# The RWKV recurrence of a diffusion step: 64x64 blocks per head in diagonal quarters of TensorE, written out without its loop

## The reference, cut to what matters

```python
def wkv7_scan(r, w, k, v, kk, a, s0, reverse):
    def step(s, inp):
        r_t, w_t, k_t, v_t, kk_t, a_t = inp
        sa = jnp.einsum('bhvk,bhk->bhv', s, -kk_t)
        s = s * w_t[:, :, None, :] + sa[..., None] * (kk_t * a_t)[:, :, None, :] + v_t[..., None] * k_t[:, :, None, :]
        return s, jnp.einsum('bhvk,bhk->bhv', s, r_t)
    xs = tuple(jnp.moveaxis(t, 1, 0) for t in (r, w, k, v, kk, a))
    s_fin, y = lax.scan(step, s0, xs, reverse=reverse)
    return jnp.moveaxis(y, 0, 1), s_fin
```

## Time and profile before

| | us |
|---|---|
| median of 3 runs (6167.9 to 6171.29) | 6169.99 |
| span of the profiled execution | 6159.2 |
| PE busy | 4924.3 (80%) |
| DVE busy | 1753.6 (28%) |
| ACT busy | 898.5 (15%) |
| POOL busy | 494.2 (8%) |

### The profile page before, as it was taken

How to read it: one execution, slowest core, us unless ns; L and a number is a source line. 1 busy time by engine, 2 the same in 40 slices (tenths; PEclk the granted TensorE clock), 3 DMA queues, 4 the chain that set the end, 5 groups by cost and what they waited for, 6 DMA issues and landing times. The chain is left out here.

```text
span 6159.2 us, 76147 instructions
## 1 busy us (share of the span) xinstructions
PE 4924.3 (80%) x31726; PEld 4331.8 (70%) x31726; DVE 1753.6 (28%) x2068; ACT 898.5 (15%) x1195; POOL 494.2 (8%) x284
## 2 busy tenths in 40 slices
PE   4799999963289999963516579984999999999990
PEld 1799999951189999951106434454999999999990
DVE  3200100037533333335466623334000000000006
ACT  0111111112122222212422300000000000000000
POOL 1100000003211011111101000000000000000003
PEclk6899999975589999986755789985999999999995
DMA  8422222113311111125853162225777777777755
GB/s 316 140 64 67 65 71 64 58 54 117 110 29 31 27 28 32 32 73 206 306 146 80 49 222 82 82 90 193 262 251 264 240 260 251 261 261 249 264 175 219
DMA packets 517520, 891.70 MB, mean 145 GB/s; under 512 B 149102, under 2 KB 321642, under 8 KB 498394
## 3 DMA queue, kind: packets, MB, share of 16 engines
q1 hardware_dynamic: 478596, 794.19, 38.1%
q0 software_dynamic: 5808, 38.93, 2.5%
q10 hardware_dynamic: 32964, 56.31, 2.5%
HBM read 747.98 MB, written 141.35 MB: 144 GB/s over the span
## 5 line engine op out<-in xcount | busy, mean ns | idle before, releaser
L2430 PE MATMUL ex_bank<-ex_xT,ex_ring 128*128 128x144 f32 x8192 | 1029.6, 287 | 9.5 <-DVE ex_yT L2538 9.0
L2430 PEld LDWEIGHTS ex_bank<-ex_xT,ex_ring 128*128 128x128 f32 x8192 | 1013.2, 190 | 13.8 <-issue 12.2
L379 PE MATMUL feat_acc<-proj_hH,feat_wH 128*128 128x384 f32 x2112 | 706.7, 335 | 12.6 <-DVE feat_wL L362 12.6
L379 PE MATMUL feat_acc<-proj_hL,feat_wH 128*128 128x384 f32 x2112 | 706.4, 334 | 0.0
L379 PE MATMUL feat_acc<-proj_hH,feat_wL 128*128 128x384 f32 x2112 | 706.4, 334 | 0.0
L2444 PE MATMUL ex_bank<-ex_act,ex_ring 128*128 128x144 f32 x4096 | 537.3, 297 | 0.0
L2444 PEld LDWEIGHTS ex_bank<-ex_act,ex_ring 128*128 128x128 f32 x4096 | 533.8, 200 | 0.6
L2059 PE MATMUL op_acc<-op_w,op_yT 128*128 128x512 f32 x1152 | 497.3, 595 | 25.2 <-DMA op_w<-in_w_out 25.2
L2059 PEld LDWEIGHTS op_acc<-op_w,op_yT 128*128 128x128 f32 x1152 | 219.8, 191 | 302.2 <-issue 302.2
L379 PEld LDWEIGHTS feat_acc<-proj_hH,feat_wH 128*128 128x128 f32 x2112 | 397.2, 188 | 13.0 <-DVE feat_wL L362 13.0
L379 PEld LDWEIGHTS feat_acc<-proj_hL,feat_wH 128*128 128x128 f32 x2112 | 397.3, 188 | 0.0
(11 more groups left out here) (403 smaller groups left out, 6220.9 us busy)
## 6 DMA issues: line engine op xcount, KB each, us to landing
ex_ring<-in_w_gate SPq DMA_DIRECT2D x256, 512.0 KB, 3.7
ex_ring<-in_w_up SPq DMA_DIRECT2D x256, 512.0 KB, 4.5
ex_ring<-in_w_down SPq DMA_DIRECT2D x256, 512.0 KB, 4.4
lru_wq<-in_w_mod SPq DMA_DIRECT2D x64, 1024.0 KB, 11.6
proj_raw<-in_w_in SPq DMA_DIRECT2D x43, 1024.0 KB, 5.5
mod_slab<-in_w_mod SPq DMA_DIRECT2D x8, 4096.0 KB, 31.0
scratch_FEAT<-feat_out ACTq DMA_DIRECT2D x43, 576.0 KB, 2.8
rr_bdt<-scratch_RW SPq DMA_DIRECT2D x288, 64.0 KB, 2.4
```

Source lines behind the costliest of these rows:

```text
L379: last = pe.matmul(acc[k][:, g, 0:SEG], a[:, k, t, :], b[:, t, cols], start=t == 0 and j == 0, stop=t == KT - 1 and j == 2)
L2430: last = pe.matmul(bank[b][:, n * C:(n + 1) * C], ring[:, k % RING, h * FE + f * P:h * FE + (f + 1) * P], xT[:, k, :], start=k == 0 and n ...
```

## The change

Each head is computed as its own 64x64 block. A matmul of head h uses partitions 64h to 64h + 63 of its operands and `tile_position=(64 * h, 64 * h)`, so the two heads of a pair use two diagonal quarters of the array and write the two halves of the same PSUM columns. The zeros are gone: buffers are 128x256 per direction, `bdt` becomes `src`, loaded by 8 DMAs a chunk and never cleared. Products are joined where both halves fit one bank: T and Tt, X and Y of a level, kT and bT (now `kb`), each with one eviction of 512 columns; there are 19 products instead of 25. Transposes become matmuls with a unit matrix `eye` as the moving operand. POOL makes X1 and Y1 in one operation. The masks become compact, with their content the same. The loop over pairs of chunks is written out on every engine. The exchange of states uses one DMA each way.

```diff
 PRODUCTS = [
-    ("T", "dve", ""), ("Tt", "dve", ""), ("Bt", "dve", ""), ("A2", "dve", ""), ("W2", "dve", "T Tt"),
-    ("X2", "act", "W2 Tt"), ("Y2", "act", "W2 Tt"), ("W4", "dve", "X2"), ("X4", "act", "W4 Y2"), ("Y4", "act", "W4 Y2"),
-    ("W8", "dve", "X4"), ("X8", "act", "W8 Y4"), ("Y8", "act", "W8 Y4"), ("W16", "dve", "X8"), ("vT", "act", ""),
-    ("X16", "act", "W16 Y8"), ("Y16", "act", "W16 Y8"), ("W32", "dve", "X16"), ("R", "dve", "Bt vT -S"),
-    ("Y32", "act", "W32 Y16"), ("kT", "act", ""), ("U", "dve", "R Y32"), ("bT", "act", ""), ("Yo", "act", "U A2 vT -S"),
-    ("S", "dve", "U bT kT vT"),
+    ("T", "dve", ""), ("Bt", "dve", ""), ("A2", "dve", ""), ("W2", "dve", "T"),
+    ("XY2", "act", "W2"), ("vT", "act", ""), ("W4", "dve", "XY2"), ("XY4", "act", "W4"),
+    ("W8", "dve", "XY4"), ("XY8", "act", "W8"), ("W16", "dve", "XY8"),
+    ("kb", "act", ""), ("XY16", "act", "W16"), ("R", "dve", "Bt vT -S"), ("W32", "dve", "XY16"),
+    ("Y32", "act", "W32"), ("U", "dve", "R Y32"), ("Yo", "act", "U A2 vT -S"), ("S", "dve", "U kb vT"),
 ]
...
-        masks = s.sb("masks", [P, 2, 9, P])
+        eye = s.sb("eye", [P, RC])
+        masks = s.sb("masks", [P, 2, 9, RC])
         pc = s.sb("pc", [P, 2, NJ_A, T // RC])
-        S = s.sb("S", [P, 2, 4, P])
-        Stmp = s.sb("Stmp", [P, 2, 4, P])
-        bdt = s.sb("bdt", [P, 2, 4, 2, 4, P])
+        S = s.sb("S", [P, 2, 4, RC])
+        Stmp = s.sb("Stmp", [P, 2, 4, RC])
+        src = s.sb("src", [P, 2, 2, 4, 4, RC])
         rt = s.sb("rt", [P, 2, 2, 4, RC])
-        names = "X1 Y1 Tt Bt A2 bT kT vT W X Y R U"
-        buf = {n: s.sb(n, [P, 2, 4, P]) for n in names.split()}
+        buf = {n: s.sb(n, [P, 2, 4, RC]) for n in "Tt Bt vT W R U".split()}
+        for n in "XY1 XY A2 kb".split():
+            buf[n] = s.sb(n, [P, 2, 2, 4, RC])
         yo = s.sb("yo", [P, 2, 2, 4, RC])
-        sio = s.sb("sio", [P, 2, 4, P])
-        pre = s.sb("pre", [P, 2, 3, 4, P])
+        sio = s.sb("sio", [RC, 16, RC])
+        pre = s.sb("pre", [P, 2, 2, 4, RC])
+        strict = s.sb("strict", [P, 2, 4, RC])
...
-                def pairs_loop(eng, body):
-
-                    if pairs == 1:
-                        body(0)
-                    else:
-                        with eng.Fori(0, pairs) as i:
-                            body(i)
+                def each_pair(body):
+                    for i in range(pairs):
+                        body(i)
...
-                            for h in range(2):
-                                hs = slice(64 * h, 64 * h + 64)
-                                for ar in range(4):
-                                    sp.dma_start(bdt[hs, slot, ar, g, :, hs],
-                                                 d["RW"][ar, g].rearrange("(j p) t -> p j t", p=P)[hs, :, t0]
-                                                 ).then_inc(slot_in[slot], 16)
+                            for ar in range(4):
+                                sp.dma_start(src[:, slot, g, ar], d["RW"][ar, g].rearrange("(j p) t -> p j t", p=P)[:, :, t0]
+                                             ).then_inc(slot_in[slot], 16)
                             sp.dma_start(rt[:, slot, g], d["RT"][g].rearrange("(j p) t -> p j t", p=P)[:, :, t0]
                                          ).then_inc(slot_in[slot], 16)
                     for slot in range(2):
                         load(slot, slot)
-                    if pairs > 1:
-                        with sp.Fori(1, pairs) as i:
-                            for slot in range(2):
-                                for g in range(2):
-                                    sp.wait_ge(product[g], NP_ * (2 * (i - 1) + slot + 1))
-                                load(2 * i + slot, slot)
+                    for i in range(1, pairs):
+                        for slot in range(2):
+                            for g in range(2):
+                                sp.wait_ge(product[g], NP_ * (2 * (i - 1) + slot + 1))
+                            load(2 * i + slot, slot)
...
                                 for c in range(4):
+                                    for h in range(2):
+                                        hs = slice(64 * h, 64 * h + 64)
+                                        B = lambda nm: buf[nm][hs, g, c, :]
+                                        half = lambda nm, z: buf[nm][hs, g, z, c, :]
+                                        I = lambda ar: src[hs, slot, g, ar, c, :]
+                                        X, Y = xy[hs, g, 0, c, :], xy[hs, g, 1, c, :]
+                                        r = rt[hs, slot, g, c, :]
+
+                                        def mm(lhs, rhs, a=True, b=True, z=0):
+                                            o = out[hs, (4 * z + c) * RC:(4 * z + c + 1) * RC]
+                                            return pe.matmul(o, lhs, rhs, start=a, stop=b, tile_position=(64 * h, 64 * h))
+                                        if name == "T":
+                                            mm(I(KKT), I(BH))
+                                            last = mm(I(BH), I(KKT), z=1)
+                                        elif name == "Bt":
+                                            last = mm(I(KH), I(KKT))
+                                        elif name == "A2":
+                                            mm(I(BH), r)
+                                            last = mm(I(KH), r, z=1)
+                                        elif name == "vT":
+                                            last = mm(I(V), eye[hs, :])
+                                        elif name == "kb":
+                                            mm(I(KH), eye[hs, :])
+                                            last = mm(I(BH), eye[hs, :], z=1)
+                                        elif name[0] == "W":
+                                            last = mm(B("Tt"), X)
+                                        elif name[0] == "X":
+                                            mm(Y, B("W"))
+                                            last = mm(B("W"), Y, z=1)
+                                        elif name == "Y32":
+                                            last = mm(B("W"), Y)
+                                        elif name == "R":
+                                            mm(I(KKT), S[hs, g, c, :], True, False)
+                                            last = mm(B("Bt"), B("vT"), False, True)
+                                        elif name == "U":
+                                            last = mm(Y, B("R"))
+                                        elif name == "Yo":
+                                            mm(B("U"), half("A2", 0), True, False)
+                                            mm(B("vT"), half("A2", 1), False, False)
+                                            last = mm(S[hs, g, c, :], r, False, True)
+                                        elif name == "S":
+                                            mm(half("kb", 1), B("U"), True, False)
+                                            last = mm(half("kb", 0), B("vT"), False, True)
                                 last.then_inc(product[g], 1)
...
-                                    dst = buf[name if name[1] == "T" else name[0]]
-                                    act.activation(dst[:, g].rearrange("p c t -> p (c t)"), out[:], ACT.Copy
+                                    act.activation(flat2(buf["kb" if name == "kb" else "XY"][:, g]), out[:], ACT.Copy
                                                    ).then_inc(took["act"][g], 1)
...
-                        for k, name in enumerate(("X1", "Y1")):
-                            for g in range(2):
-                                if k:
-                                    pool.wait_ge(masked[g], n + 1)
-                                else:
-                                    wait_taken(pool, g, n, "T")
-                                pool.tensor_tensor(buf[name][:, g], pre[:, g, 2 - k], rep(ident[:]), ALU.add).then_inc(eyed[g], 1)
-                    pairs_loop(pool, lambda i: [step(i, slot) for slot in range(2)])
+                        for g in range(2):
+                            wait_taken(pool, g, n, "T")
+                            pool.tensor_tensor(buf["XY1"][:, g].rearrange("p z c t -> p (z c) t"), pre[:, g].rearrange("p z c t -> p (z c) t"),
+                                               rep(eye[:], 8), ALU.add).then_inc(eyed[g], 1)
...
-                                    inc(dve.tensor_tensor(pre[:, g, 2], o4, rep(masks[:, g, M_ONE]), ALU.mult))
-                                elif name == "Tt":
-                                    dve.tensor_tensor(pre[:, g, 1], o4, rep(masks[:, g, M_ONET]), ALU.mult)
-                                    dve.tensor_tensor(pre[:, g, 0], o4, rep(masks[:, g, M_STRICT]), ALU.mult).then_inc(masked[g], 1)
-                                    dve.wait_ge(masked[g], n + 1)
```

(56 more changed lines are left out.)

68 lines of the change are left out of this document (16 added, 52 removed).

## The result

The changed kernel takes 5793.79 us in the median of 4 runs (5788.88 to 5805.51), the kernel before 6170.64; the ratio is 0.9401, 95% interval 0.9380 to 0.9421. The forecast was 5760 us. The profiled execution after has a span of 5803.7 us. The traces show that two errors went against each other: the recurrence gained some 18 us more than was summed, and a stage that the change does not touch lost 68 us. Part of the closeness is luck of another kind: the profiled span before lies 10.8 us under the median, and this was added to the forecast, while the profiled execution after is the slowest of its four and its span lies 9.9 us over the median. Between the two spans the forecast missed by 55.5 us (-411 said, -355.5 measured), between the medians by 34.

A forecast was written before the change was run, and what follows sets the result against it. TensorE's order of work was taken to bound the recurrence, not evictions or loads. Sample -354, prompt -39, start, first loads and exchange -18 took 6159.2 to 5748; plus 10.8 for the median, 5760 us, range 5715 to 5985.

The forecast's parts named there:

- start and first load: Ahead of the first chunk: buffer clearing falls away, 6.5 us, and TensorE waits 9 instead of 13.9 us, 4.9 us.
- sample: Recurrence over the sample's 16 chunks: 32.7 us each, 523 us against 877.1, so -354 us.
- The pace: Recurrence matmuls: two quadrants overlap, 29 ns per record instead of 111.7; 960 records make 27.8 us per chunk.
- The waits: Recurrence chunks: evictions no longer hide, so TensorE waits 4.9 us per chunk, giving a chunk of 32.7 us.
- The loop: Sample's recurrence loop, written out: 7 returns of 7.6 us go, 53 us.
- Code supply: Sample's chunks: about 160 code packets instead of 78, taken to cost 0; upper bound 608 us in place of 523.
- The loop and its code: Step on writing out the recurrence loop: 53 us of returns saved, constant fetching of new code taken as 0.
- Turns: Rival, recurrence: quadrants take turns, 58 ns a record, evictions hidden, kernel about 6172 us; chance 0.08.
- clock: Rival, recurrence: TensorE's clock falls to its lower level, 58 us per chunk, kernel 6215 us; chance 0.04.
- drain: Rival, recurrence: each switch of quadrant empties the array, 169 ns, kernel 7640, or 6540 at a quarter; chance 0.05.
- sequencer: Rival, recurrence: each instruction costs the sequencer time, kernel 7050, or 6250 by the skill's figure; chance 0.02.
- The case of code supply: Rival, recurrence: code every 3.8 us or half-hidden handovers, 38 to 40 us per chunk, 5855 to 5890 us; chance 0.16.

The follow-up runs named there:

- burst a: Changed kernel plus idle waits, with 32 unread matmuls behind the sample's last chunk, two heads' quadrants in turn, one bank: 29.5 ns a record.
- c: Same kernel with added unread matmuls behind the sample's last chunk, here 64 records on one quadrant alone: 58.4 ns a record.
- hmajor: Changed kernel with 200 fulfilled waits in the exchange, and within each product all matmuls of head 0 before head 1: 5982.47 us, 0.9714.
- double_xy: Changed kernel with 200 fulfilled waits in the exchange, and ACT copying each joint X and Y product first into an unread buffer: 5752.13 us, 0.9348.
- before_unrolled: Kernel before with only its loop over pairs of chunks written out, plus 143 fulfilled TensorE instructions in the exchange: 6117.65 us, 0.9929.
- before_shift60: Kernel before with 60 more TensorE instructions (120 fulfilled waits) in the exchange of states: 6132.80 us, 0.9963.

## Why the prediction was right, and where it was not

By its own terms, with the stretches above and the earlier trace rows:

| term | said | measured |
|---|---|---|
| start and first load | -11.4 | -14.8 (3.4 of it ahead of the stage) |
| prompt | -39 | -39.8 |
| exchange | -6.6 | -8.2 |
| sample | -354 | -369.9 |
| behind the recurrence | 0 | +77.2 |
| profiled span | -411 | -355.5 |
| median over the span | +10.8 | -9.9 |

- **The pace: right.** 29 ns was half of the 58 worked out for one quadrant, and that two overlap was taken over from the column groups of the modulation's rows; the burst a has 29.5, the chunk 29.1. c shows the other bound, 58.4, which had been worked out as 58. That the order of the heads carries it was given as the reason, and hmajor bears it out.
- **The waits: right in kind, a little large.** 4.9 us a chunk were said, 3.8 measured (31.7 - 27.9); that is the 16 us by which the sample's term is off. double_xy speaks for the handover, since an eviction that ends later costs a quarter of itself there; which term of my sum of waits was too large was not measured.
- **The loop: right.** 53 us said; 52.3 in before_unrolled. That some 35 us of it come from where the loop lay (before_shift60) was not seen.
- **Code supply: right for the recurrence, wrong in scope.** Straight code costs nothing visible at 61 TensorE instructions per us (31057 in 507.2 us; 2.3 us of "issue"). It came to 122 packets, against 78 in the earlier trace rows and the 160 that I had put. But the step "The loop and its code" asked only what the code costs where it runs. It left out that 31 thousand added instructions move all later code, by 157 within a packet, and that the experts' loop of 1682 instructions is kept or not by that. This step failed: a term of +68 us that the sum doesn't have. It is more than the whole miss, 55.5 us between the spans and 34 between the medians.
- **The rivals.** Turns, clock, drain and sequencer are out: 29 ns, a clock of 0.99, and two records started every 58 ns with their loads. The case of code supply came out in a place where it wasn't looked for, in the experts and not in the recurrence.
- **What stays open.** Of the 77.2 us behind the recurrence 68 are the experts. The other 9 lie mostly in the SSD stage, whose parts differ by 5 to 10 us between kernels that share its code; no run was made for that. The 68 us of the experts are placed by the stretches: TensorE's idle time grew by 41 us, all of it before the line of the returns (9.5 us before, 50.3 after), and its busy time by 27 (1729.2 to 1756.2), of which 23 are in that line (1029.6 and 1052.3). After 12 of the 14 returns the first 32 records take 5.85 instead of 4.18 us, after one 6.79, together some 23 us more: the lower clock behind the wait.

```profile
L2430 PE MATMUL ex_bank<-ex_xT,ex_ring 128*128 128x144 f32 x8192 | 1029.6, 287 | 9.5 <-DVE ex_yT L2538 9.0 <-ACT ex_xT L2468 0.4
```

```profile
L2427 PE MATMUL ex_bank<-ex_xT,ex_ring 128*128 128x144 f32 x8192 | 1052.3, 290 | 50.3 <-issue 49.2 <-DVE ex_yT L2535 0.6 <-ACT ex_xT L2465 0.4
```

(The costliest groups' row of the experts' line, before and after: busy us, mean ns, idle before.)

## What to carry to other kernels

A change in one stage moves the code of all later ones. Compare every later stage's length, its "issue" waits and its code packets between the two traces, and where a large loop has begun to read its code anew at each return, idle instructions in a wait ahead of it can bring it back (5794 to 5734 us here, and 5718 with a better order of products). Two heads of 64 channels belong in two diagonal quadrants, and in alternation: the same matmuls in blocks of one head cost 45.4 us a chunk instead of 31.6.

## What the runs showed of the hardware that I had not expected

- TensorE's loop body of 1682 instructions is kept between turns at some places and read anew at others: 13 or 14 packets against 139 or 140, and 62 to 70 us for 14 returns, 4.4 to 5.0 us each. Of that about 2.9 are wait, and from the second return on about 1.7 are records at the lower clock behind it.
- A body of 1917 instructions, the old recurrence's, was kept at none of three places; its return cost one wait of about 1.9 us (13.2 and 12.7 us for 7), or two of 1.60 and 2.77 us with a slow restart, by where it began.
- Two diagonal quadrants into one bank run as fast as into two, 29.5 and 29.1 ns a record. Changing head every 8 records still gives 40.0 ns against 58.4 for one quadrant alone.
- Two copies of ACT in a row overlap: of 256 columns they start 0.29 us apart and last 0.38, of 512 columns 0.49 apart and last 0.60.
